# The input projection as seven block products per pair of column tiles

## The reference

```python
n = rmsnorm(h, g_in)
z = n @ w_in                       # 2048 x 6152: q, k, v, f (8), ga, u, gs
logf = log_sigmoid(fl + b_f)       # forget gate of 8 heads
att = fox_attention(q, cumsum(logf), k, v)
ssm = s5(u, ...)                   # 64 groups x 16 channels, 64 complex states each, then gelu and GLU
h = h + concat(att * silu(ga), ssm * silu(gs)) @ w_out
h = h + rmsnorm(pe @ w_pe) * sigmoid(h @ w_pg)
y = rmsnorm(h, g_final)            # outputs: y, k, v, logf, last states of prompt and sample
```

## Time and profile before

| | |
|---|---|
| median of 3 runs | 2588.84 us (2579.69 to 2591.14) |
| profiled execution, first to last instruction | 2583.1 us |
| TensorE busy | 2398.8 us (93%) |
| weight loads (beside the matmuls) | 2267.0 us (88%) |
| VectorE busy | 1358.0 us (53%) |
| ScalarE busy | 486.3 us (19%) |
| GpSimd busy | 373.5 us (14%) |
| norm ends, projection starts | 79.8 us |
| attention issues its first load | 1330.1 us |
| bytes read and written in HBM | 219 and 86 MB |

### The profile page before, as it was taken

One profiled execution on the slowest core, in us unless ns is written; L12 is line 12 of the kernel. 1 busy time (PEld: TensorE's weight loads), 2 busy tenths in 40 slices (PEclk: granted clock), 3 DMA queues, 4 the chain that ended last, 5 costly groups with the idle time before them and its releaser, 6 DMA issues. The chain is left out here.

```text
span 2583.1 us, 41868 instructions
## 1 busy us (share of the span) xinstructions
PE 2398.8 (93%) x14931; PEld 2267.0 (88%) x14931; DVE 1358.0 (53%) x3010; ACT 486.3 (19%) x1052; POOL 373.5 (14%) x461
## 2 busy tenths in 40 slices
PE   5899999999999999999978886797999999999996
PEld 5889999999999999999967775696888888999996
DVE  6652322322322288888848774754444665434663
ACT  7110010100000010112136552412000113000112
POOL 1011011011011011212133330600000110001110
PEclk8899999999999999999989997998999999999998
DMA  7233323323323244444456543444445436434333
GB/s 267 72 100 85 89 80 85 89 80 85 89 80 85 67 119 128 119 127 119 112 165 184 169 141 117 166 137 157 133 120 159 122 102 194 128 103 124 103 109 104
DMA packets 367917, 310.86 MB, mean 120 GB/s; under 512 B 41777, under 2 KB 320337, under 8 KB 365361
## 3 DMA queue, kind: packets, MB, share of 16 engines
q1 hardware_dynamic: 334672, 213.33, 29.6%
q0 software_dynamic: 17568, 44.93, 5.9%
q10 hardware_dynamic: 15616, 51.85, 5.3%
HBM read 219.44 MB, written 86.26 MB: 118 GB/s over the span
## 5 line engine op out<-in xcount | busy, mean ns | idle before, releaser
L97 PE MATMUL acc<-n_hi,w_in_hi 128*128 128x352 f32 x2352 | 518.3, 328 | 9.9 <-DVE w_in_lo L135 9.9
L97 PE MATMUL acc<-n_hi,w_in_lo 128*128 128x352 f32 x2352 | 508.6, 324 | 0.0
L97 PE MATMUL acc<-n_lo,w_in_hi 128*128 128x352 f32 x2352 | 508.3, 324 | 0.0
L1885 PE MATMUL post_acc<-region_hi,w_post_hi 128*128 128x272 f32 (+1 forms) x1536 | 418.2, 326 | 23.4 <-DVE region_lo L1994 19.2
L1885 PE MATMUL post_acc<-region_hi,w_post_lo 128*128 128x272 f32 (+1 forms) x1536 | 415.9, 325 | 0.0
L1885 PE MATMUL post_acc<-region_lo,w_post_hi 128*128 128x272 f32 (+1 forms) x1536 | 415.0, 325 | 0.0
L97 PEld LDWEIGHTS acc<-n_hi,w_in_hi 128*128 128x128 f32 x2352 | 398.8, 190 | 15.1 <-DVE w_in_lo L135 10.6
L97 PEld LDWEIGHTS acc<-n_hi,w_in_lo 128*128 128x128 f32 x2352 | 405.4, 189 | 0.0
L97 PEld LDWEIGHTS acc<-n_lo,w_in_hi 128*128 128x128 f32 x2352 | 401.1, 189 | 0.0
L130 DVE CAST w_in_hi<-w_raw 128x1024 fp32r<-128x1024 f32 x98 | 63.7, 690 | 483.9 <-PE acc L97 426.0
L1885 PEld LDWEIGHTS post_acc<-region_hi,w_post_hi 128*128 128x128 f32 x1536 | 258.4, 189 | 48.7 <-issue 16.0
(11 more groups left out here) (328 smaller groups left out, 2902.4 us busy)
## 6 DMA issues: line engine op xcount, KB each, us to landing
w_raw<-in_w_in_dram SPq DMA_DIRECT2D x98, 512.0 KB, 5.1
w_raw<-in_w_out_dram SPq DMA_DIRECT2D x64, 512.0 KB, 4.8
w_raw<-in_w_pg_dram SPq DMA_DIRECT2D x64, 512.0 KB, 4.7
zT<-z_out ACTq DMA_DIRECT2D x32, 528.0 KB, 2.7
uT<-z_out ACTq DMA_DIRECT2D x16, 528.0 KB, 2.8
eT<-e_out ACTq DMA_DIRECT2D x16, 528.0 KB, 2.9
x_in<-in_x_prompt_dram SPq DMA_DIRECT2D x8, 1024.0 KB, 6.9
xT<-xT POOLq DMA_DIRECT2D x8, 1024.0 KB, 6.1
```

The lines of the kernel that those rows point to most:

```text
L97: mm = pe.matmul(acc[:, c, 0:CH], w[:, k, :], a[:, k, c * CH:(c + 1) * CH], start=(k == 0 and n == 0), stop=(k == kt - 1 and n == 2))
L1885: mm = pe.matmul(acc[b][:, c, 0:width], w[:, k, :], a[region][:, k, start:start + width], start=(k == 0 and n == 0), stop=(k == KD - 1 and ...
```

## The change

Norm and projection become one stage, `stage_front`. The tokens go in two passes of 528 (HN). In a pass each of 24 pairs of column tiles (256 columns) is one block product: weights cut into four blocks A11, A12 (rows, that is features, in halves of 8 blocks; columns in halves of 128) and so on, tokens into two quarters of 264 (QN). Seven products of 8 blocks of features x 3 matmuls x 264 tokens stand in place of eight (Strassen's scheme in Winograd's form). The seven activation sides are computed once per pass (`t_subs`, `t_high_parts`, `t_low_parts`); of the weight side, A21, A11, A22 and A12 are overwritten one after the other by four sums, on GpSimd (`sums`), once the low part of what they overwrite has been taken. High parts are now made on ScalarE (`high`), low parts on VectorE (`low`), three buffers of each, two products ahead. Results are put together from PSUM: copies on ScalarE (`drain`), three additions on VectorE (`combine`), two on GpSimd (`difference`, `corner`). Every weight is loaded twice, 1 MB at a time into three raw buffers.

Norm of the first pass stands ahead; that of the second is woven into pairs 0 to 4 and goes through a scratch nT. The constants of 4 groups go into each of pairs 7 to 22, the recurrence of 4 groups into pairs 29 to 44, and their stores are issued by SP and ScalarE, no longer by GpSimd. The table of rotations is built to length 34 once, on VectorE, for all groups, and lengthened for each four groups on GpSimd (`turns(q)`). The recurrence does 8 scans for four groups instead of 16, with a second swap by DMA after them. The forget gate runs after pairs 23 and 24 with 264-column matmuls. All loops are written out, none runs on the chip. The gate gs is now in zT in token order; the side stage reads it with another stride. Attention and output are the same but for where the weight buffer is allocated.

The core of the diff ("..." marks what is left out):

```diff
+KH = KD // 2
+HN = T // 2
+QN = T // 4
+QJ = QN // L
+RF = 34
+ROWS_OF = ([(0, P), (P, P), (2 * P, P), (3 * P, P), (4 * P, HN - 4 * P)],
+           [(HN, P), (HN + P, P), (HN + 2 * P, P), (HN + 3 * P, T_PROMPT - HN - 3 * P), (T_PROMPT, T_SAMPLE)])
...
+        FACTOR = ("A11", "A22", "A12", "A21", "A11", "A22", "A12")
+        ACT_SIDE = (0, 6, 1, 3, 4, 5, 2)
+        BANK = (0, 1, 0, 2, 3, 1, 2)
+        OPENS = (True, True, False, True, True, False, False)
...
+            def load_w(p, h):
+                if p > last:
+                    return
+                if h == 0 and p >= 2:
+                    sp.wait_ge(lo_done, 7 * (p - 1))
+                if h == 1 and p >= 1:
+                    sp.wait_ge(lo_done, 7 * (p - 1) + 5)
+                    sp.wait_ge(s_done, 4 * p)
+                s = raw_slot(p, h)
+                col = pair_column(p % NP)
+                sp.dma_start(w_raw[s][:], w_in[:, h * KH:(h + 1) * KH, col:col + 2 * P]).then_inc(w_loaded[s], 16)
...
+            def load_rot(q):
+                if q >= NPB:
+                    return
+                b = q % 2
+                if q >= 2:
+                    sp.wait_ge(v_used, q - 1)
+                sp.dma_start(rot[b][:, :, :, 0:RF], d["rotF"][:, :, q * PB:(q + 1) * PB]).then_inc(rot_loaded[b], 16)
...
+            for p in range(2 * NP):
...
+                if RECUR <= p <= LAST_RECUR:
+                    load_u(p - RECUR)
+                if p:
+                    store_z(p - 1)
...
+                load_w(p + 1, 1)
+                if RECUR <= p <= LAST_RECUR:
+                    load_ws(p - RECUR + 1)
+                    load_rot(p - RECUR + 1)
+                load_w(p + 2, 0)
...
+                if p == NP - 1:
+                    sp.wait_ge(prod_done, 7 * NP)
+                    for kp in range(KH):
+                        load_nb(kp)
+                if RECUR <= p <= LAST_RECUR:
+                    load_ro(p - RECUR)
+                    if p > RECUR:
+                        store_y(p - RECUR - 1)
...
+            def sums(p, which):
+
+                a11, a12, a21, a22 = (block_of(p, x) for x in ("A11", "A12", "A21", "A22"))
+                if which == 0:
+                    for h in range(2):
+                        pool.wait_ge(w_loaded[raw_slot(p, h)], raw_count(p, h))
+                    TT_(a21, a21, a22, ALU.add).then_inc(s_done, 1)
+                    return
+                pool.wait_ge(lo_done, 7 * p + which)
+                pool.wait_ge(s_done, 4 * p + min(which, 2))
+                if which == 1:
+                    TT_(a11, a21, a11, ALU.subtract).then_inc(s_done, 1)
+                else:
+                    x = a22 if which == 2 else a12
+                    TT_(x, x, a11, ALU.subtract).then_inc(s_done, 1)
...
+            def difference(p):
+
+                pool.wait_ge(drained, 4 * p + 4)
+                if p:
+                    pool.wait_ge(pool_combined, 2 * p)
+                TT_(vv[:], p5s[:], p4s[:], ALU.subtract).then_inc(pool_combined, 1)
+
+            def corner(p):
+
+                pool.wait_ge(combined, 3 * p + 2)
+                pool.wait_ge(pool_combined, 2 * p + 1)
+                TT_(z_view(z2, p, 1), z_view(z2, p, 0), like(vv[:], p), ALU.add).then_inc(pool_combined, 1)
+
+            def turns(q):
+
+                b = q % 2
+                r = rot[b]
+                pool.wait_ge(rot_loaded[b], 16 * (q // 2 + 1))
+                for m, n in ((33, 33), (66, 65)):
+                    er, ei = (r[:, s, :, m:m + 1].to_broadcast([P, PB, n]) for s in range(2))
+                    br, bi = r[:, 0, :, 1:1 + n], r[:, 1, :, 1:1 + n]
+                    t0, t1 = rot_t[:, 0, :, 0:n], rot_t[:, 1, :, 0:n]
+                    TT_(t0, er, br, ALU.mult)
+                    chain.link(TT_(t1, ei, bi, ALU.mult))
+                    chain.link(TT_(r[:, 0, :, m + 1:m + 1 + n], t0, t1, ALU.subtract))
+                    TT_(t0, er, bi, ALU.mult)
+                    chain.link(TT_(t1, ei, br, ALU.mult))
+                    x = TT_(r[:, 1, :, m + 1:m + 1 + n], t0, t1, ALU.add)
+                    if m == 33:
+                        chain.link(x)
+                    else:
+                        x.then_inc(rot_ready, 1)
+
+            for kp in range(KH):
+                t_subs(0, kp)
+            sums(0, 0)
+            sums(0, 1)
+            for p in range(2 * NP):
+                if p:
+                    corner(p - 1)
+                if p == NP:
+                    for kp in range(KH):
+                        t_subs(1, kp)
+                sums(p, 2)
+                sums(p, 3)
+                if p == RECUR - 1:
+                    pool.wait_ge(arena_open, 3)
+                    nc.gpsimd.memset(h_prev[:, :, 0:1], 0.0)
+                    turns(0)
+                if RECUR <= p < LAST_RECUR:
+                    turns(p - RECUR + 1)
+                difference(p)
+                if p < last:
+                    sums(p + 1, 0)
+                    sums(p + 1, 1)
+            corner(last)
...
-            def tile(n, b, it, hooks=None):
-                pe.wait_ge(W.split[1], n + 1)
-                pe.wait_ge(evacuated[b], it)
-                gemm_tile(pe, acc[b], W.hi[b], W.lo[b], G["n_hi"], G["n_lo"], KD, hooks=hooks) \
-                    .then_inc(W.gemm_done, 1)
...
+            def product(p, r):
+                n, s = 7 * p + r, slot_of(p, r)
+                out = acc[:, BANK[r], 0:QN]
+                pe.wait_ge(lo_done, n + 1)
+                if r in (0, 1, 3, 4) and p:
+                    if r == 0:
+                        pe.wait_ge(drained, 4 * p - 1)
+                    else:
+                        pe.wait_ge(combined, 3 * (p - 1) + {1: 2, 3: 3, 4: 1}[r])
+                if r in (2, 5, 6):
+                    pe.wait_ge(drained, 4 * p + {2: 1, 5: 2, 6: 4}[r])
+                for k in range(KH):
+                    if r == 0 and p in (0, NP):
+                        pe.wait_ge(t_ready, (p // NP) * KH + k + 1)
+                    hi, lo = t_act[:, k, 0, ACT_SIDE[r]], t_act[:, k, 1, ACT_SIDE[r]]
+                    for m, (w, a) in enumerate(((w_hi[s], hi), (w_hi[s], lo), (w_lo[s], hi))):
+                        mm = pe.matmul(out, w[:, k, :], a, start=(OPENS[r] and k == 0 and m == 0),
+                                       stop=(k == KH - 1 and m == 2), skip_group_check=True)
+                mm.then_inc(prod_done, 1)
...
+            for p in range(2 * NP):
+                for r in range(7):
+                    if p < NT and r == 5:
+                        spread(1, p)
+                    if p < NT and r == 6:
+                        turn_x(1, p)
+                    if p == 5 and r == 4:
+                        turn_raw()
+                    if PREP <= p <= LAST_PREP:
+                        if r == 1:
+                            turn_c(p - PREP)
+                        if r == 4:
+                            turn_state(p - PREP)
+                        if r == 6:
+                            kernels(p - PREP)
...
+                    if RECUR <= p <= LAST_RECUR and r == 3:
+                        states(p - RECUR)
+                    if RECUR < p <= LAST_RECUR + 1 and r == 4:
+                        readout(p - RECUR - 1)
+                    product(p, r)
+                if p in (NP - 1, NP):
+                    gates(p - NP + 1)
...
+            def high(n):
+
+                if n >= 7 * 2 * NP:
+                    return
+                p, r = n // 7, n % 7
+                if n >= 3:
+                    act.wait_ge(prod_done, n - 2)
+                if r < 3:
+                    h = 0 if r == 0 else 1
+                    act.wait_ge(w_loaded[raw_slot(p, h)], raw_count(p, h))
+                else:
+                    act.wait_ge(s_done, 4 * p + r - 2)
+                nc.scalar.copy(w_hi[n % 3][:], block_of(p, FACTOR[r])).then_inc(hi_done, 1)
+
...
+            def swap(done, count, landed, q):
+
+                act.wait_ge(done, count)
+                act.dma_start(v[0:ST, 1], v[ST:P, 0]).then_inc(landed, 16)
+                act.dma_start(v[ST:P, 1], v[0:ST, 0]).then_inc(landed, 16)
...
+            for p in range(2 * NP):
+                for j in range(7):
+                    if j in (1, 2, 3, 4):
+                        drain(p, j - 1)
+                    if p == NP and j == 0:
+                        snap_gates(0)
+                        for kp in range(KH):
+                            t_high_parts(1, kp)
+                    if p == NP + 1 and j == 0:
+                        snap_gates(1)
+                    high(7 * p + j + 2)
+                    extra(p, j)
...
+                link(TT_(tt[:, 0], b12, b11, ALU.subtract))
+                TT_(tt[:, 1], b22, tt[:, 0], ALU.subtract).then_inc(t_sub_dve, 1)
+
+            def t_low_parts(half, kp):
+                n = half * KH + kp
+                tt = (tt_a, tt_b)[half][kp % 2]
+                dve.wait_ge(t_high, n + 1)
```

(75 more changed lines are left out.)

1549 lines of the change are left out of this document (896 added, 653 removed).

## The result

The changed kernel takes 3031.65 us (3026.8 to 3038.07, 4 runs) against 2587.29 us: a ratio of 1.172, 95% interval 1.169 to 1.175. I had forecast slower, 2834 us, with a range of 2590 to 2960: the direction held, the size did not. Its profiled execution spans 3025.1 us, and its attention issues its first load at 1774.20 us, where it was 1330.1. Behind that point both take the same, 1251 and 1253 us. So all 442 us are in the stage that the diff replaces.

A forecast was written before the change was run, and what follows sets the result against it. TensorE bounds the old stage; in the new one the VectorE-GpSimd lock decides. TensorE 1089, start 105, early pairs 31 + 27, constants 109, recurrence 142, middle 39 + 25, end 8: 1575 us against 1330, hence 2834 us, range 2590 to 2960.

The forecast's parts named there:

- TensorE's sum: TensorE's own work in the new stage: 1089 us, at 121.7 ns a matmul and 20.45 us a bare pair.
- the start: Norm of the first token half and operand sums before the projection: 105 us, from 90 to 110.
- some 115 us: What the stage would win if nothing were late, stated after TensorE's sum of 1089 us.
- Constants pairs: Pairs 7 to 22: TensorE waits before state transposes and kernels, 29.3 us a pair, 109 us of waiting in 16 pairs.
- that follows the end of product 2. From there: drain 0.39: Constants pairs: chain from product 2 through drain, high, low and input block, 5.4 us against one product of 2.92.
- rival (d): Its claim is not in the text given; chance 0.04, and the forecast range leaves it out.
- The lock: VectorE and GpSimd run one after the other; recurrence pairs 29 to 44 take 32 us, 142 us of waiting.
- the signs that I had named: If right: low parts of 2.5 us and more, recurrence pairs about 32, constants pairs 27 to 31, middle idle some 39.
- Pairs 0 to 6: First seven pairs: waits of 31 us in pairs 0 to 4 and 27 us in pairs 5 and 6.
- Middle: Operand rebuild between token halves: 9.5 us per two block rows, four times, TensorE idle 39 us (28 to 45).
- (b): Rival: faster, all waits inside pairs vanish because high and low parts run two products ahead; 2466 us, chance 0.15.
- (a): Rival: lock mostly hidden, only in-order waits stay, 46 us of them in the recurrence; 2676 us, chance 0.19.

The follow-up runs named there:

- e1: Changed kernel with SyncE issuing the stores of the previous pair's z before the nine block loads in constants pairs, not behind them; 2920.68 us.
- e3: Changed kernel with GpSimd's four weight sums of a pair cut to the first column of each block, timing only; 2813.36 us.
- e4: Changed kernel with useless filling matmuls in constants pairs, 56 ahead of the state transposes and 32 ahead of the kernels; 3027.35 us.
- e11: Changed kernel with the exchange of e1 and shorter filling, 28 matmuls ahead of the state transposes and 14 ahead of the kernels; 2914.48 us.
- e6: Changed kernel with VectorE's low parts of a block row put ahead of the next row's sums, between the token halves; 3025.07 us.
- e9: Changed kernel with the four short scans of each recurrence pair left out, timing only; 3029.22 us.

## Why the prediction was right or wrong

**The bound of the stage, TensorE's sum, the start.** Right: 122 ns a matmul, bare pairs of 20.4 us, 107 us for 105. The "some 115 us" that the stage would win with nothing late is 128 by the prediction's own terms (1330 - 1089 - 105 - 8); nothing else hangs on it.

**Constants pairs: wrong, and most of the error.** The step that failed is "that follows the end of product 2. From there: drain 0.39": the chain was begun at the end of product 2 with the drain as its first link, and the wait of that drain for its buffer was put at nothing, without a reason. It measured 96.6 us in 14 pairs, 6.9 each. I had priced the DMA issues as time on a queue that has room, and for the recurrence pairs only. What I did not ask was which wait stands ahead of the stores: `load_block` waits for a step of the current pair, nine loads follow, and the single buffer `z1` makes the drain wait for the store behind them. Pair 22, which has no such loads, takes 31.5 us in the same profile (907.4 to 938.9). That is 111 of the 198 us, shown by e1. Two things make it up: the late store, and the collision before the kernels, 2.90 us for 0.757 in all 16 pairs, which e1 removed along with it in 14 of them. Leaving out GpSimd's sums alone (e3) gave 75 us in the same pairs, so the causes overlap and their gains must not be added.

With the store put right, 497.0 us stand against a forecast of 16 x 29.3 = 469: 28 of the 144 remain. TensorE's two waits are then 92 us, under the 109 of the forecast; what the forecast had nothing for are the products, 32 us over 2.80 each. Filling the gaps took 18 of these away and gave 7, so even this rest is not simply the clock's, and it stays open. The forecast's own chains were also added up wrongly: their terms give 5.04 and 4.54 us where 5.4 and 4.85 stand, 0.7 us of waiting a pair too much.

**The clock: seen, and small as a price.** The time came out over 2960, where rival (d) stood at 0.04, and products behind waits took up to 5.2 us, at a granted clock of 0.50. They are not what put it there. The slow products are some 53 us in the constants pairs; restoring the clock there made the stretch 16 us shorter in e4 and 7 in e11, and the kernel's median 4 and 6. Nor are GpSimd's steps slow by themselves: at their shortest, the twelve steps of the table, eight of which read an operand by broadcast, take 0.41 to 0.47 us (132 elements) and 0.61 to 0.74 (260), where I had taken 0.47 and 0.74.

**The lock: right in size, in part by luck, the turns shown in part.** 142 forecast, 154 measured. But I had added 30.4 to 33.6 us of common work a pair; counted from the trace it is 28.8, and the other 3.9 us of the pair are waits in which neither engine does such work. The groups by shape of VectorE in the changed kernel, count, busy us and mean ns of one:

```profile
L1173 DVE TENSOR_TENSOR w_lo<-w_raw_f,w_hi 128x1024 fp32r<-128x1024 f32 x336 | 482.4, 1441 | 322.9 <-ACT w_hi L947 322.4 <-DVE rot_f L1396 0.2
...
L1421 DVE TENSOR_TENSOR_SCAN v<-rho,va 128x4 f32<-128x4 f32 x64 | 87.0, 1359 | 0.0
...
L1421 DVE TENSOR_TENSOR_SCAN v<-rho,va 128x128 f32<-128x128 f32 x64 | 40.7, 638 | 0.0
...
L1182 DVE TENSOR_TENSOR u<-acc,p1s 128x264 f32<-128x264 f32 x48 | 20.7, 431 | 138.3 <-PE acc L726 138.2
```

Low parts take 1.44 us on average where the earlier trace rows have 1.218, and 1.256 with the sums cut down (e3); a scan of four columns, 0.14 us before, takes 1.36, and 0.29 in e3; the second step of `ca` takes 2.90 us where the earlier trace rows have 0.757, and 0.77 in e3. The addition with one input in PSUM (line 1182) takes 0.43 us, also in the 15 of its 48 cases that fall wholly inside one of GpSimd's sums. So low parts, scans and that multiplication, each with two inputs from SBUF, became longer beside GpSimd's sums, and the addition from PSUM did not. The earlier trace rows show it for a subtraction alone: that all of the multiplications and scans in my 15.3 us exclude GpSimd's work was my assumption, and no run shows the 33.6 us added up from it; what the runs showed in its place is the lengthening just given and the 28.8 us. Of the signs that I had named, recurrence pairs of about 32 us came; low parts of 2.5 us and more are only 19 of 336, and 231 still take 1.26 or less.

**Pairs 0 to 6.** 66 for 58, sized well.

**Middle: 26 us short.** I had one load and 5.5 us of work for two block rows with two buffers. VectorE's list asks for the next row's sums ahead of this row's low parts, so load and work stand in series, 7.5 us a row and not 4.75: 22 us over eight rows. The exchange in e6 gave back 10 of them.

**Rivals.** (b), faster, needed under 123 us of waits; there were over 500. (a) took the lock as hidden and put 46 us of waiting into the recurrence pairs; there were 154, and leaving out the sums gave 113 of them. That run takes GpSimd's own time away as well, so it refutes (a)'s number and not by itself its reason.

## What to carry to other kernels

When work is woven into a shorter stage, write out for every single-buffered tile who must free it, on which queue that store stands, and what the instructions ahead of it on that queue wait for: a DMA queue with much idle time can still be late in every turn, here by 5.3 us in pair 15. Where VectorE and GpSimd are both busy, as in these recurrence pairs, count GpSimd's work and VectorE's on two inputs from SBUF as that of one engine and compare the sum with TensorE's time (28.8 against 23.1 us here). Where it is larger, find out by a run what order can still give: in the recurrence pairs here it was at most 1.9 us a pair, in the constants pairs 7.3. A fallen clock behind a wait is first a sign of the wait; filling the wait gave 4 and 6 us here, where removing its cause gave 111.

## What the hardware showed that I had not expected

VectorE and GpSimd took turns, and short instructions waited behind long ones: the second step of `ca`, 0.757 us before, ended 0.6 us behind a sum of 2.80 us and took 2.90. Over the 16 recurrence pairs the eight scans last 7.5 us on average and at most 9.1, as in pair 35; with the sums cut down (e3) 2.8. First the row of e3's pair 34, then pair 35 of the changed kernel with GpSimd's instructions beside it:

```profile
1200.92 3.48 DVE L1421 TENSOR_TENSOR_SCAN v<-rho,va 128x128 f32<-128x128 f32 x8
```

```profile
1376.29 9.10 DVE L1421 TENSOR_TENSOR_SCAN v<-rho,va 128x128 f32<-128x128 f32 x8
...
1376.94 2.52 POOL L611 TENSOR_TENSOR w_raw_f<-w_raw_f 128x1024 f32<-128x1024 f32 x1
1379.61 2.38 POOL L616 TENSOR_TENSOR w_raw_f<-w_raw_f 128x1024 f32<-128x1024 f32 x1
1381.95 0.92 POOL L640 TENSOR_TENSOR z<-z,vv 128x264 f32<-128x264 f32 x1
1382.84 5.92 POOL L619 TENSOR_TENSOR w_raw_f<-w_raw_f 128x1024 f32<-128x1024 f32 x2
```

The first two sums here take 2.52 and 2.38 us, where the shortest in the whole trace takes 2.34, so up to there it is VectorE that pays. The last row holds two sums, 2.53 and 3.43 us: the second pays as well, beside a low part. Over the stage the sums take 2.53 to 2.69 us on average, by line, and up to 4.40. Nor is it shortness that draws the wait: with the short scans gone (e9) the long ones take 1.66 us each instead of 0.64.
